# Output projection of token tile 0 issued inside the two attentions of the first block, in a two-block transformer kernel on one core

## The reference, cut to what matters

```python
def masked_softmax(s, mask):
    s = jnp.where(mask, s, NEG)
    s = s - jnp.max(s, axis=-1, keepdims=True)
    e = jnp.exp(s) * mask
    return e / jnp.maximum(jnp.sum(e, axis=-1, keepdims=True), 1e-30)

# layer 0: 12 heads of 64, in 2 groups; three branches, mixed by gates
    return g[..., 0:1] * o_cmp + g[..., 1:2] * o_slc + g[..., 2:3] * o_win
...
# layer 1: 12 heads, scores with a forget term
        s = s + dcum[:, :, lo:hi, None] - dcum[:, :, None, :hi]
        p = masked_softmax(s, jnp.arange(hi)[None, :] <= t[:, None])
...
def memory_attention(q_mem, mem, g_mem, w_mem_kv):       # 4 heads of 64, 256 memory rows, no mask
    kv = (rms_norm(mem, g_mem) @ w_mem_kv).reshape(B, M, 2, N_MEM_HEADS, HEAD_DIM)
    s = jnp.einsum('bthd,bmhd->bhtm', q_mem, kv[:, :, 0]).astype(jnp.float32) * HEAD_DIM ** -0.5
    p = jax.nn.softmax(s, axis=-1).astype(kv.dtype)
    o = jnp.einsum('bhtm,bmhd->bthd', p, kv[:, :, 1])
...
# in both layers
        o_mem = memory_attention(q_mem, mem, mem_norm[l], w_mem_kv[l])
        x = x + jnp.concatenate([o_mix, o_mem], axis=-1) @ w_o[l]
        x = x + conv_ffn(rms_norm(x, ffn_norm[l]), w_up[l], conv_w[l], conv_b[l], w_down[l])
```

## Time and profile before

| | us |
|---|---|
| median of 3 runs | 2189.39 |
| lowest, highest | 2187.23, 2189.82 |
| the profiled execution: its own time | 2190.59 |
| its span, first to last instruction | 2188.7 |

### The profile page before, as it was taken

One profiled execution on the slowest core, in us unless ns is written; L12 is line 12 of the kernel. 1 busy time (PEld: TensorE's weight loads), 2 busy tenths in 40 slices (PEclk: granted clock), 3 DMA queues, 4 the chain that ended last, 5 costly groups with the idle time before them and its releaser, 6 DMA issues.

```text
span 2188.7 us, 29543 instructions
## 1 busy us (share of the span) xinstructions
PE 2024.3 (92%) x9709; PEld 1110.9 (51%) x9710; DVE 997.6 (46%) x2209; ACT 680.8 (31%) x1085; POOL 45.5 (2%) x79
## 2 busy tenths in 40 slices
PE   8879999999899999999999888998998998888887
PEld 4534777744567776645443333333684433333333
DVE  2263888421558735334544333434315443333335
ACT  1142100011510002132455444444201554444444
POOL 2000000000000000000000000000000000000001
PEclk9869999999899999999999999999999999999999
DMA  8501899443159744311899999999655899999996
GB/s 289 189 23 68 330 349 345 174 150 150 53 195 372 278 157 164 137 56 43 308 420 423 422 409 422 422 422 388 235 192 199 329 422 423 422 422 422 422 423 260
DMA packets 78478, 619.86 MB, mean 283 GB/s; under 512 B 9632, under 2 KB 9952, under 8 KB 15664
## 3 DMA queue, kind: packets, MB, share of 16 engines
q1 hardware_dynamic: 67824, 540.51, 61.9%
q0 software_dynamic: 6912, 66.33, 8.1%
q10 hardware_dynamic: 3648, 11.89, 1.3%
HBM read 605.06 MB, written 13.63 MB: 283 GB/s over the span
## 4 chain that ended last, share of the span: by engine, by line
PE 65%; DMA 26%; DVE 4%; ACT 2%; issue 2%; DVEq 0%; SPq 0%; ACTq 0%
PE ps L834 26%; DMA big<-in_w_up 24%; PE ps L1044 14%; PE ps L1218 11%; PE ps L1056 7%; PE ps L1220 2%; PE ps L848 2%; PE ps L1191 1%; ACT big L1705 1%; DMA big<-in_w_gate 1%; DMA big<-in_dense 0%; PE ps L1202 0%; DVE big L2100 0%; DMA big<-in_w_down 0%; PE ps L1066 0%
## 5 line engine op out<-in xcount | busy, mean ns | idle before, releaser
L1218 PE MATMUL ps<-big,hT 128*32 128x512 f32 x3072 | 702.0, 609 | 85.9 <-ACT big L1705 74.4
L1220 PE MATMUL ps<-big,hT 128*32 x1536 | 701.1, 609 | 0.0
L1705 ACT COPY big<-big 128x1024 f32 x384 | 396.3, 1046 | 500.0 <-PE ps L1220 290.7
L2435 DVE TENSOR_SCALAR big<-big 128x1024 f32 x384 | 265.1, 692 | 534.8 <-PE ps L1220 318.3
L1218 PEld LDWEIGHTS ps<-big,hT 128*32 128x32 f32 x3072 | 189.1, 112 | 454.6 <-issue 242.7
L1044 PE MATMUL ps<-hT,big 128*128 128x256 f32 x1408 | 311.1, 379 | 0.0
L834 PE MATMUL ps<-big,hT 128*128 128x512 f32 (+4 forms) x792 | 299.8, 537 | 4.7 <-DMA big<-in_dense 2.4
L1044 PEld LDWEIGHTS ps<-hT,big 128*128 128x128 f32 x1408 | 266.7, 190 | 49.0 <-issue 14.8
L834 PEld LDWEIGHTS ps<-big,hT 128*128 128x128 f32 x792 | 144.0, 194 | 149.6 <-issue 140.3
L834 PE MATMUL ps<-big 64*30 64x256 f32 (+12 forms) x692 | 161.0, 521 | 21.6 <-issue 5.5
L1220 PEld LDWEIGHTS ps<-big,hT 128*32 128x32 f32 x1536 | 159.0, 112 | 5.6 <-issue 0.2
(11 more groups left out here) (328 smaller groups left out, 1235.9 us busy)
## 6 DMA issues: line engine op xcount, KB each, us to landing
big<-in_w_down SPq DMA_DIRECT2D x128, 1024.0 KB, 23.1
big<-in_w_gate SPq DMA_DIRECT2D x128, 1024.0 KB, 24.5
big<-in_w_up SPq DMA_DIRECT2D x128, 1024.0 KB, 23.5
big<-in_dense SPq DMA_DIRECT2D x52, 1536.0 KB, 8.2
big<-in_dense POOLq DMA_DIRECT2D x28, 2048.0 KB, 9.2
big<-in_dense SPq DMA_DIRECT2D x21, 2048.0 KB, 7.8
y_rows<-c_res ACTq DMA_DIRECT2D x30, 384.0 KB, 7.0
big<-in_dense SPq DMA_DIRECT2D x5, 1024.0 KB, 8.4
```

Of the source, the lines that this page charges most:

```text
L1218: nc.tensor.matmul(ps[g * SLOTS:(g + 1) * SLOTS, bank, :], xT[:, k, g * SLOTS:(g + 1) * SLOTS], side[:, g - 1, quarter % 2, at:at + BW], s ...
L1220: return nc.tensor.matmul(ps[0:SLOTS, bank, :], xT[:, k, 0:SLOTS], experts3[:, bass.ds(here, 1), kind * CH + row:kind * CH + row + BW] .re ...
L1705: nc.scalar.copy(side[:, 1, quarter % 2, :], experts3[:, bass.ds(there, 1), lo:lo + QW] .rearrange("p a n -> p (a n)")).then_inc(s["side2_ ...
L2435: ts(side[:, 0, quarter % 2, :], experts3[:, bass.ds(there, 1), lo:lo + QW].rearrange("p a n -> p (a n)"), 1.0, None, mult).then_inc(s["si ...
```

## The change

The 16 products of tile 0 in layer 0, and 12 of the 16 in layer 1, no longer stand behind the attention but inside it, one at the end of an iteration of PE's loop, into banks 6 (half 0) and 7 (half 1). The table `FILL` says which iteration issues which product: in nsa iterations 8 to 11 (slices 6 and 7) and 14 to 25 (slices 0 to 5), in fgt iterations 6 to 17 (slices 0 to 5). Each waits until ACT has copied the group that it reads into `oT` (`out_done`). The memory heads, whose outputs are slices 6 and 7, now lead the nsa list (so tile 1's mixer heads come last, and `SLOT0` shifts the `probsT` slots by two). PE takes both chunks of `w_o` when the attention begins and gives both back after the last product of the projection. In the projection itself tile 0 needs four products in layer 1 and none in layer 0; then come the 16 of tile 1, and the residual adds, squares and turns go tile by tile instead of half by half.

```diff
...
-        ATT = {"nsa": nsa_units() + mem_units(2 * NH, B_QM, B_KM),
+        ATT = {"nsa": mem_units(2, B_QM, B_KM) + nsa_units(),
                "fgt": forget_units() + mem_units(NH, F_QM, F_KM), "mla": mla_units()}
 
+        SLOT0 = {"nsa": 2, "fgt": 0, "mla": 0}
+        FILL = {"nsa": {8 + i: (i // 2, 6 + i // 2, i % 2) for i in range(4)}, "fgt": {}, "mla": {}}
+        for i in range(12):
+            FILL["nsa"][14 + i] = (2 + i // 6, i // 2, i % 2)
+        for i in range(12):
+            FILL["fgt"][6 + i] = (i // 2, i // 2, i % 2)
+        TURN_BANKS = ((4, 5), (2, 3))
...
+            def out_gemm(name, norm_name, w, fills):
+
+                s, t_ = st[name], st[norm_name]
+                done = {k for _, k, _ in fills.values()}
+                for k in range(KT):
+                    for h in range(2):
+                        if k not in done:
+                            out_product(w, k, 0, h, s["banks_ready"].sem if k == w[3] else None)
+
+                def turn_of(c, h):
+                    pe.wait_ge(s["dve_evac"].sem, s["dve_evac"].at(2 * c + h + 1))
+                    raw_T(t_, lat, c, h, TURN_BANKS[c][h])
+
+                w = w[0:2] + [0, KT - 1]
+                for h in range(2):
+                    for k in range(KT):
+                        if h == 1 and k == 4:
+                            turn_of(1, 0)
+                        out_product(w, k, 1, h, s["banks_ready"].sem if k == KT - 1 else None)
+                    if h == 0:
+                        turn_of(0, 0)
+                        turn_of(0, 1)
+                used(2)
+                turn_of(1, 1)
...
-            def attention(name):
+            def out_product(w, k, c, h, done=None):
+
+                mm(ps[:, 6 + h if c == 0 else h, :], oT[:, k, c * P:(c + 1) * P], w[h][:, k, :], k == w[2], k == w[3], done)
+
+            def out_chunks(first, last):
+                return [take().rearrange("p (k n) -> p k n", k=KT) for _ in range(2)] + [first, last]
+
+            def attention(name, o_name=None):
...
+                def fill(i):
+
+                    group, k, h = FILL[name][i]
+                    pe.wait_ge(s["out_done"].sem, s["out_done"].at(group + 1))
+                    out_product(w, k, 0, h, st[o_name]["banks_ready"].sem if k == w[3] else None)
...
                     if LAG <= i < n + LAG:
                         probs_T(i - LAG)
+                    if i in FILL[name]:
+                        fill(i)
+                return w
...
-                                pe.wait_ge(t_["turned_v"].sem, t_["turned_v"].at(k // 2 + 2))
+                                pe.wait_ge(t_["turned_v"].sem, t_["turned_v"].at(k // 4 + 3))
...
-            squares_after(st["wo0"]["dve_evac"], "normF0", by_half)
+            squares_after(st["wo0"]["dve_evac"], "normF0", by_tile)
...
+                for c in range(TC):
+                    for h in range(2):
+                        i = 2 * c + h
+                        out = lat(c)[:, h * BW:(h + 1) * BW]
+                        v.wait_ge(s["banks_ready"].sem, s["banks_ready"].at(i + 1))
+                        tt(out, out, ps[:, 6 + h if c == 0 else h, :], add).then_inc(s["dve_evac"].sem, 1)
+                    for h in range(2):
+                        turn(norm_name, 2 * c + h, c, h, TURN_BANKS[c][h], gain, S)
...
```

More of the change, by code:

```diff
@@ L916, in token_scales @@
                     .then_inc(s["scales_ready"].sem, 1)
-            def out_gemm(name, lhs, T, turned=None):
-                s = st[name]
-                i = 0
-                for half in range(2):
-                    w = take()[:, :].rearrange("p (k n) -> p k n", k=KT)
-                    for c in range(T):
-                        if turned is not None and i == 2 * T - 1:
-                            for q in range(T):
-                                pe.wait_ge(s["dve_evac"].sem, s["dve_evac"].at(q + 1))
-                                raw_T(turned, lat, q, 0, 4 + q)
-                        for k in range(KT):
-                            mm(ps[:, i % BANKS, :], lhs(k, c), w[:, k, :], k == 0, k == KT - 1,
-                               s["banks_ready"].sem if k == KT - 1 else None)
-                        i += 1
-                    used()
+            def out_gemm(name, norm_name, w, fills):
[19 more added lines that the diff above has]
+                turn_of(1, 1)
             def heads(name, blocks, rows, after_two=None, bank0=0):
@@ L1356, in _ @@
             after(pe, "cmpatt")
-            attention("nsa")
+            w = attention("nsa", "wo0")
             after(pe, "nsa")
-            def last_turns(name, norm_name):
-                s = st[name]
-                for q in range(TC):
-                    pe.wait_ge(s["dve_evac"].sem, s["dve_evac"].at(TC + q + 1))
-                    raw_T(st[norm_name], lat, q, 1, 6 + q)
-            out_gemm("wo0", lhs_o, TC, st["normF0"])
-            last_turns("wo0", "normF0")
+            out_gemm("wo0", "normF0", w, FILL["nsa"])
             ffn("ffn0", "normF0")
@@ L1406, in _ @@
             after(pe, "headsB")
-            attention("fgt")
+            w = attention("fgt", "wo1")
             after(pe, "fgt")
-            out_gemm("wo1", lhs_o, TC, st["normF1"])
-            last_turns("wo1", "normF1")
+            out_gemm("wo1", "normF1", w, FILL["fgt"])
             ffn("ffn1", "normF1", ctx_turns)
@@ L1820, in squares_after @@
                 root(norm_name, rstd_x)
-            by_half = [(c, h) for h in range(2) for c in range(TC)]
             by_tile = [(c, h) for c in range(TC) for h in range(2)]
-            squares_after(st["wo0"]["dve_evac"], "normF0", by_half)
+            squares_after(st["wo0"]["dve_evac"], "normF0", by_tile)
             token_scales("normF0")
@@ L2010, in residual_turned @@
                 s = st[name]
-                for i in range(2 * TC):
-                    half, c = i // TC, i % TC
-                    out = lat(c)[:, half * BW:(half + 1) * BW]
-                    v.wait_ge(s["banks_ready"].sem, s["banks_ready"].at(i + 1))
-                    tt(out, out, ps[:, i % BANKS, :], add).then_inc(s["dve_evac"].sem, 1)
-                    if i == 2 * TC - 2:
-                        for q in range(TC):
-                            turn(norm_name, q, q, 0, 4 + q, gain, S)
-                for q in range(TC):
-                    turn(norm_name, TC + q, q, 1, 6 + q, gain, S)
+                for c in range(TC):
[6 more added lines that the diff above has]
+                        turn(norm_name, 2 * c + h, c, h, TURN_BANKS[c][h], gain, S)
                 t_ = st[norm_name]
```

11 lines of the change are left out of this document (7 added, 4 removed).

## The result

| | runs | median us | ratio to before (95% interval) |
|---|---|---|---|
| before, beside it | 5 | 2188.58 | |
| changed kernel | 5 | 2176.52 | 0.9945 (0.9927 to 0.9963) |
| changed kernel, on another chip | 6 | 2176.03 (before 2190.41) | 0.9932 (0.9916 to 0.9949) |

A forecast was written before the change was run, and what follows sets the result against it. PE was busy 92% of the span, but in the attentions idled 22.6 us, mostly behind DVE. Gains of 13.8 (first attention and projection) and 3.8 us (second) made 17.6 off 2190.59: 2173.0, median 2172, range 2164 to 2184.

The forecast's parts named there:

- The projections: Both output projections, to the first up product: 16.6 us for the first and 20 for the second.
- By itself the order of the heads gives some 3.4: First attention: memory heads cost 10.0 us at the end and 6.5 at the start, so moving them first gives some 3.4.
- the bounds: Total: 2162 us with all hidden and the order's 3.4, 2189 at full cost without it, 2214 all at 1.2 GHz.
- the full-price rival: Both attentions: every product costs in full where it stands, only the order of heads gives 3.4 us; 2186 us, chance 0.08.
- The walk of the first attention: First attention along PE's order: 14.7 + 13.3 + 36.3 = 64.3 us, plus 1.5 for low clock, 65.8.
- The rule of place: Tile-0 pairs: a product between two turns costs nothing, one ahead of the next scores its full 0.87 us.
- The second attention: Second attention, iterations 6 to 17: the moved products cost 6.2 us in sum.
- The table for the second network: Second network's start: two ring chunks compete with the table DVE waits for; between 0 and 1.7 us, taken as 0.
- The signs I had named: Attentions 64 to 67 and 44 to 46 us; clock 1.00 after memory heads; wrong if 0.50 over 10 us in the first.
- The clock does not rise: Attentions: some 25 us walked at 2.4 GHz run at 1.2, losing 11 us; gain 6.6, time 2183 us, chance 0.15.
- All is hidden: Both attentions: the odd products fall into idle time too; 2163 us, chance 0.12.
- Slower, with the clock held low: Both attentions: products run at 1.2 GHz and hold the clock low, 27 us slower, 2217 us; chance 0.05.

The follow-up runs named there:

- order_only: The changed kernel with no product moved: memory heads first, projection by tile behind each attention; 2193.62 us, ratio 1.0022 to before.
- drain: The changed kernel with the last four products of the first attention at iterations 26 to 29, in its end; 2170.57 us, one run.
- even: The changed kernel with the first attention's 16 products two at a time in even iterations, between a pair's two turns; 2175.12 us, one run.
- release: The changed kernel with the first chunk of w_o given back after its own half, before the last turns and products; 2174.43 us, ratio 0.9944 to before.
- odd: The changed kernel with the first attention's 16 products two at a time in odd iterations, ahead of the next scores; 2185.15 us, one run.
- placed: The changed kernel with first-attention products in twos between turns, four in the end, and early return of the first weight chunk; 2169.02 us, ratio 0.9912 to before.
- fgt_only: The old order of heads with only layer 1's twelve products moved, projection by tile in both layers; 2188.38 us, ratio 0.9997 to before.
- memlast: The changed kernel with memory heads last and only twelve first-layer products moved, one to an iteration at 16 to 27; 2179.68 us, ratio 0.9962 to before.
- placed_last: The changed kernel with memory heads last, twelve first-attention products in twos between turns, four behind it, early chunk return; 2172.71 us, ratio 0.9918 to before.

## Why the prediction was right, and where its working was not

The total lay inside the range, 4.5 us above the forecast, and the direction and the main mechanism held. The terms one by one:

**The projections: right.** I had 16.6 and 20 us, and measured 16.76 and 20.20. PE now waits 0.87 us for the last residual add, where it waited 0.34, and the way to the first up product is still as walked. A projection by tile costs 0.6 (30.49 against 29.85), where I had 0.4.

**"By itself the order of the heads gives some 3.4": this step failed.** It costs 2.6 us (order_only). Two things were wrong in it. I set the walked start of 14.7 us (measured 14.6) against 8.15 for "the first two tile-0 pairs"; but at 131.95 three pairs stand behind PE, and what the start is to be held against ends at 128.80, after 5.0. With the right count the start costs 9.7 and the end saves 10.0: nothing. And the end saves only 6.8, since I walked it at 11.1 us and it takes 14.3 there: PE idles between its last turns, the clock is low, and the outputs take 5.1 us and not 3.6. The walk itself does not use the 3.4; the bounds and the full-price rival do, and both were too kind by 6 us.

**The walk of the first attention: 4.9 us too short at full clock, 3.4 with the 1.5 I had added.** Start 15.6 (walked 14.7), tile 0 14.6 (13.3), tile 1 up to the last pair 25.9 (25.2), end 13.1 (11.1). The largest part is the end, the mis-sized term: 1.5 us of its 2.0 are the outputs at 1.2 GHz. I had let the clock stay high there, although show it low behind tile 1 before, too; drain confirms it by removing it. The 0.9 of the start are its low clock, 10.3 us and not the 5 I had walked; where it was low for 6.8, the start took 14.6. (Two slips in that walk hardly matter: 125.35 + 0.7 + 1.3 is 127.35, not 127.1, and the 1.56 us for two memory scores spans a fall of the clock, they take 1.13 at 2.4 GHz.) In tile 0 the first and the last pair take 3.98 and 3.97 us and not 3.2, as each waits 0.58 and 0.17 for DVE; the second takes 3.24. Tile-1 pairs take 4.29 and not 4.0, as the idle of 0.27 remains between one product and the second turn. The forecast that PE would have no gap there was wrong for the changed kernel and right for even (3.80).

**The rule of place: confirmed in layer 0.** A product between the turns falls into DVE's time and one ahead of the scores stands in the loop: 3.80, 4.29 and 5.16 us a pair. It was what I used to price the products. In layer 1 no run changed the places.

**The second attention: right in kind, 6.2 forecast, 5.4 measured** at equal low clock (42.65 - 37.26 with 10.3 us low, and 44.43 - 39.02 with 13.7). Against before it cost only 3.7, because 3.5 us less of it are at 1.2 GHz, and that is luck: without any product (order_only) they are gone, too. It gave 1.8 us and balanced about half of the missing 3.7 us of layer 0 (13.8 forecast, 10.1 measured; layer 1 3.8 and 6.0).

**The table for the second network: priced 0 to 1.7, taken 0, measured 1.2.** The table took 11.4 us to land instead of 7.6 (its DMA issue in either profile), with two ring chunks released beside it. DVE waited 9.07 instead of 5.34 us, 3.7 more, which is the 3.7 for one chunk that I had named as the most, without a row for it. Release removes PE's wait and leaves the table 0.9 us later than before.

**The signs I had named.** The direction of the total was right, but several signs were not. The first attention took 69.18 us (64 to 67 forecast) and the second 42.67 (44 to 46). The clock was not at 1.00 from the end of the memory heads on: it fell at 185.20. And it was at 0.50 for 13.7 us of the first attention, more than the 10 that I had said would show the prediction wrong. The sign was set too tight: the start alone, which the change does not fill, was low for 10.3, and the whole is less than half of the 30.7 us of before. Tile-1 pairs stayed under 4.5 us, and PE waited neither for a chunk nor, in the pairs, for `out_done`.

**The rivals.** "The clock does not rise" is out: the low clock in both attentions fell from 44.4 to 23.9 us. The page "TensorE: Matmul & The Clock Gate" of the Trainium skill, section "A second HAM failure mode: psum-queue depth-cycling", says that short pauses of PE between groups of matmuls make its clock swing. I had counted it against the change. The traces fit the rule and turn it round: in order_only, with pauses and no products, the clock falls four times in the first attention, in the changed kernel twice, and in drain, with the last pauses filled, once. Odd has the same 16 products but keeps the pauses ahead of the second turns, and its clock falls four times again. From the third pair of tile 0 on it is low for 13.7 us in odd, 6.8 in even and 23.9 in order_only, so both the products and their places count. "All is hidden" is out for the changed kernel (both attentions are longer), though placed has it in the first attention, which is shorter there than before (64.30 against 66.15). "Every product in full" is out by even, where two products cost 0.13 us a pair; for products ahead of the scores it is nearly right (1.49 of 1.74 in odd). "Slower, with the clock held low" did not come.

What stays open: the sum of the four stages is 16.1 us, and the medians show 12.1 and 14.4. The two profiled executions differ by 15.8 us, but they are no typical pair: that of before (2190.59) took longer than all of the five runs beside it, and that of the changed kernel (2174.81) was the fastest of its five. The new wait takes 1.2 of the difference. It is not all of it: in release, which lacks the wait, the stages give 17.0 us and the medians 11.8, and in fgt_only the 6.0 us of layer 1 do not appear in the total at all. In seven of the eleven changed profiles the stretch between the first projection and the second attention is 339.8 to 340.0 us instead of 338.0 to 338.3, as the clock is low for 6.8 us near its end and not for 3.4. The changed kernel showed this in both of its profiles; before, even, odd, memlast and placed_last did not. What sets it, and what makes the rest of the program differ by a few us, was not tried.

## What to carry to other kernels

A matmul moved into a latency-bound loop costs by its place: ahead of the wait for the slower engine it is nearly free (0.13 us for two products of 0.87), behind that wait and ahead of what that engine needs next it costs nearly all of its time (1.49). Where the wait is long enough, put two in the first place rather than one in each, and keep some for the end of the pipeline, where no next pair fills the waits. Price the clock with the idle time: a product that fills pauses can give back more than it takes, so an attention with 16 products in it ran in less time than without them.

## What the runs showed of the hardware

- The attention with 16 more products (placed, 64.30 us) is shorter than without them (order_only, 68.75), with 13.6 us against 30.7 at 1.2 GHz. With the same products but the pauses left in (odd) the clock fell four times as in order_only, with the pauses filled once or twice.
- In the second attention the first 3.4 us more at 1.2 GHz cost 1.8 us (39.02 against 37.26 without products, 44.43 against 42.65 with them), a further 3.4 only 0.4 (44.84).
- How long the clock stays low at the start of an attention differed between kernels whose order there is the same: 6.8, 10.3 or 13.6 us in the first, each step adding 0.95 us (14.64, 15.59, 16.54), and 10.2, 13.7 or 17.1 us in the second, with PE busy 7.64 of 10.20 us in the changed kernel. No run here says what decides it.
- The rest of the program, which no edit touches but for the table's wait, took between 1556.5 and 1565.7 us in single profiles. A gain of a few us must be read in its own stage; a median of a few runs does not show it.
